# Norms with root and reciprocal per token on partitions, all normalised tiles on VectorE, and the modulation turned in batches

## The chip, the cores and the metric

One core of one Trainium2 chip runs the kernel in one launch. The metric is the device time in microseconds (us); the median of the runs before is 1482.4.

## The reference

Two layers of one trunk work on 256 latent tokens and 256 context tokens of width 1024. Each half of a layer begins with a norm, whose result is modulated; the six modulation vectors of a layer come from two condition vectors (one for latent, one for context tokens):

```python
cond_x = silu(c); cond_c = silu(c_ctx)
for l in range(2):
    mod_x = split(cond_x @ w_mod[l] + b_mod[l], 6)     # 1024 x 6144; mod_c from cond_c alike
    hx = rmsnorm(x, g_norm1[l]) * (1 + mod_x[1]) + mod_x[0]     # hc alike
    px = hx @ w_in[l]       # 3088 columns: mLSTM, differential attention, conv
    x = x + mod_x[2] * (concat(mlstm(px), diff_attention(px), conv(px)) @ w_out[l])
    x = x + mod_x[5] * ffn(rmsnorm(x, g_norm2[l]) * (1 + mod_x[4]) + mod_x[3])
return rmsnorm(x, g_final)
# rmsnorm(x, g) = x * rsqrt(mean(x * x) + 1e-6) * g, the mean over the 1024 features of a token
```

The context stream has the same steps in layer 0 only. ffn is a dense SwiGLU (2816 wide) in layer 0 and a top-2-of-8 router with SwiGLU experts in layer 1.

## The kernel before

Activations are kept with features on partitions: X is 128 x 8 x 512, eight tiles k of 128 features, the first 256 columns the context tokens. Weights come in chunks of 256 columns (1 MB) into a ring of four slots. SyncE issues all loads of the ring in the order of one list (`chunks`), and for chunk n it waits until the last product of chunk n - 4 is through; what stands behind it in the list waits too. Products with the large weights are made from two rounded parts of each operand, three matmuls per product (L523, L818). So a weight chunk must be split before use: ScalarE or VectorE makes the leading part (L1173, L1496), VectorE the remainder (L1497, L1511). There are two buffers for leading parts, so chunk s of the split ones also waits for the products of chunk s - 2.

**A norm** (`norm`, `squared`, `deviation`, `norm_scale`): ScalarE squares each tile (L1058), VectorE sums six of the squares (L1455), TensorE adds them over partitions with two 512-wide matmuls against ones (L567, L569), which puts each token's sum on all 128 partitions. ScalarE takes the root (L1064), VectorE the reciprocal of all 512 columns (L1479). Then VectorE multiplies tiles 0, 2, 4 and 6 (L1469) and GpSimd tiles 1, 3, 5 and 7 (L2097); ScalarE applies gain and shift per half (L1078), VectorE splits the result (L1496, L1497), and TensorE begins the projections (L523) or the router (L880). In layer 1 the second norm covers the 256 latent tokens only.

**The modulation** is 24 chunks per layer. For one chunk TensorE makes 8 matmuls of 256 columns with a 32-column left side in which two columns hold the conditions (L541; 16 records), ScalarE copies the 128 x 256 result to SBUF (L1090), and TensorE turns it into columns with two matmuls against `fold` (L558, the turn; 4 records). VectorE adds the bias (L1438) and makes the gain (L1445). A chunk's turn is issued behind the next chunk's matmuls. Eight chunks come at the start, 16 in layer 0's projections (two behind each of eight weight chunks, `LATE_MOD`), eight in layer 0's attention, four each behind the column sums of the norms (0, 1), (1, 0) and (1, 1), four in layer 1's attention. Attention has 18 steps in layer 0 and 10 in layer 1; `fill` puts modulation into them on TensorE and ScalarE. ScalarE copies the rows of a norm's four chunks before its first tile of that norm.

In the ring's list, a norm's chunks surround the first weight chunk of what follows: two ahead of it, the rest behind it; then "up" (layer 0), or "mq", "cg", "ca" (layer 1). At the start the first weight chunk stands seventh, after six of the eight modulation chunks. `spin` (L530) are matmuls of constants whose result nobody reads; one spin is two records. TensorE runs its instructions in the order written, and so do the others.

After a first norm VectorE splits the tiles, then rounds constants (layer 0 only), clears the scratch, splits "mq" and "cg", waits for ScalarE's gate functions, and does the gate scans (L1533 to L1544) ahead of the remainder of "ca" (`gate_rows`).

## Time and profile before

| | us |
|---|---|
| median of 3 runs | 1482.4 (1482.19 to 1485.1) |
| the profiled execution | 1483.12 |
| its span | 1481.3 |
| TensorE busy | 1401.9 (95%) |
| VectorE busy | 994.1 (67%) |
| ScalarE busy | 642.5 (43%) |
| GpSimd busy | 205.9 (14%) |
| mean granted TensorE clock, of full speed | 0.973 |
| HBM traffic | 266 MB, 180 GB/s over the span |

All times within the kernel are counted from the start of the span. PE is TensorE's matmuls, PEld its weight loads, DVE VectorE, ACT ScalarE, POOL GpSimd, SPq SyncE's queue; L12 is a line of the kernel. A matmul on 32-bit floats appears as two records, one on rounded parts as one. The stages: first modulation and norm to 44, projections of layer 0 to 250, its attention and output to 381, norm to 406, dense stage to 755, layer 1's norm to 773, its projections to 921, attention and output to 995, norm and router to 1027, then eight trips through the experts.

### The profile page before, as it was taken

What the parts mean: (1) busy time and instruction counts of PE and PEld (TensorE: products, weight loads), DVE (VectorE), ACT (ScalarE), POOL (GpSimd) and SP (SyncE); (2) the same over time, 40 slices, a digit from 0 to 9 for tenths busy, and PEclk for the clock granted to TensorE, in tenths of its full rate; (3) what the DMA queues carried; (4) which work ended last, traced back from release to release, by engine and by line L of the source; (5) the groups of instructions that cost most, each with busy time, mean ns of one, the idle gap of its engine ahead of it and who ended that gap; (6) DMA issues with size and microseconds to landing.
All of it is one profiled execution on the core that took longest, in us unless ns stands there. A gap on an engine that the chain in (4) does not pass through costs nothing.

```text
span 1481.3 us, 20769 instructions
## 1 busy us (share of the span) xinstructions
PE 1401.9 (95%) x7796; PEld 1152.9 (78%) x7796; DVE 994.1 (67%) x1456; ACT 642.5 (43%) x1025; POOL 205.9 (14%) x150
## 2 busy tenths in 40 slices
PE   6899999989899999999988999888999999999996
PEld 3778887667688888888868888577888888878885
DVE  3755885565643443444457695755988998998996
ACT  3434334561401100010034444635677677687675
POOL 0129980000100000000011980000000000000000
PEclk9999999889999999999999989998999999999998
DMA  9254442411342322222334122238979778877940
GB/s 398 93 199 171 171 171 86 163 37 61 113 167 85 102 98 86 106 81 104 116 119 158 69 86 90 110 114 339 400 298 367 295 300 339 328 298 312 353 196 28
DMA packets 30882, 267.08 MB, mean 180 GB/s; under 512 B 3424, under 2 KB 3552, under 8 KB 4960
## 3 DMA queue, kind: packets, MB, share of 16 engines
q1 hardware_dynamic: 30816, 266.15, 47.3%
q8 instruction: 47, 0.77, 0.2%
q14 instruction: 19, 0.16, 0.0%
HBM read 265.09 MB, written 1.05 MB: 180 GB/s over the span
## 4 chain that ended last, share of the span: by engine, by line
PE 81%; DVE 9%; ACT 3%; issue 3%; DMA 3%; SPq 0%; DVEq 0%; ACTq 0%
PE ps L523 38%; PE ps L953 17%; PE ps L973 7%; PE ps L818 3%; PE ps L541 3%; PE ps L681 2%; DMA sb_arena<-mod 2%; PE ps L558 1%; PE ps L646 1%; PE ps L530 1%; PE ps L736 1%; PE ps L717 1%; DVE sb_egu_lo L1963 1%; DVE sb_w_lo L1511 1%; DVE sb_ew_lo L1974 1%
## 5 line engine op out<-in xcount | busy, mean ns | idle before, releaser
L523 PE MATMUL ps<-sb_h_hi,sb_w_hi 128*128 128x512 f32 (+1 forms) x640 | 242.4, 379 | 4.9 <-DVE sb_w_lo L1497 3.3
L523 PE MATMUL ps<-sb_h_hi,sb_w_lo 128*128 128x512 f32 (+1 forms) x640 | 240.0, 375 | 0.0
L523 PE MATMUL ps<-sb_h_lo,sb_w_hi 128*128 128x512 f32 (+1 forms) x640 | 240.0, 375 | 0.0
L953 PE MATMUL ps<-sb_egu_lo,sb_h_lo 128*128 128x512 f32 (+1 forms) x384 | 144.6, 377 | 0.0
L523 PEld LDWEIGHTS ps<-sb_h_hi,sb_w_hi 128*128 128x128 f32 x640 | 121.7, 190 | 28.3 <-DVE sb_w_lo L1497 3.9
L1496 DVE CAST sb_w_hi<-sb_arena 128x2048 fp32r<-128x2048 f32 (+1 forms) x38 | 45.5, 1197 | 141.8 <-PE ps L523 113.8
L523 PEld LDWEIGHTS ps<-sb_h_hi,sb_w_lo 128*128 128x128 f32 x640 | 121.5, 190 | 21.7
L523 PEld LDWEIGHTS ps<-sb_h_lo,sb_w_hi 128*128 128x128 f32 x640 | 121.6, 190 | 21.1
L1963 DVE TENSOR_TENSOR sb_egu_lo<-sb_arena,sb_con_r 128x1024 fp32r<-128x1024 f32 x98 | 115.3, 1217 | 15.2 <-ACT sb_con_r L1318 15.1
L1974 DVE TENSOR_TENSOR sb_ew_lo<-sb_arena,sb_ew_hi 128x1024 fp32r<-128x1024 f32 x88 | 107.1, 1217 | 11.5 <-ACT sb_ew_hi L1331 11.5
L2118 POOL TENSOR_SCALAR sb_arena<-sb_arena,sb_small 128x512 f32<-128x512 f32 (+1 forms) x60 | 104.2, 1736 | 5.9
L1331 ACT ACTIVATE sb_ew_hi<-sb_arena 128x1024 fp32r<-128x1024 f32 x88 | 91.7, 1052 | 30.1 <-PE ps L973 30.1
L1291 ACT ACTIVATE sb_arena<-ps 128x512 f32<-128x512 f32 x22 | 13.2, 599 | 202.5 <-PE ps L523 202.4
L1963 DVE TENSOR_TENSOR sb_egu_lo<-sb_arena,sb_x_r 128x1024 fp32r<-128x1024 f32 x82 | 96.5, 1217 | 0.4
L1318 ACT ACTIVATE sb_con_r<-sb_arena 128x1024 fp32r<-128x1024 f32 x96 | 96.0, 1051 | 0.0
L1511 DVE TENSOR_TENSOR sb_w_lo<-sb_arena,sb_w_hi 128x2048 fp32r<-128x2048 f32 x24 | 59.3, 2470 | 50.7 <-ACT sb_w_hi L1173 50.5
L1497 DVE TENSOR_TENSOR sb_w_lo<-sb_arena,sb_w_hi 128x2048 fp32r<-128x2048 f32 (+1 forms) x38 | 85.0, 2236 | 1.3
L953 PE MATMUL ps<-sb_con_r,sb_h_lo 128*128 128x512 f32 (+1 forms) x224 | 82.1, 367 | 3.4 <-DVE sb_egu_lo L1963 3.4
L953 PEld LDWEIGHTS ps<-sb_egu_lo,sb_h_lo 128*128 128x128 f32 x384 | 73.0, 190 | 12.6
L953 PE MATMUL ps<-sb_con_r,sb_hs_lo 128*128 128x512 f32 (+1 forms) x224 | 81.6, 364 | 0.0
L1318 ACT ACTIVATE sb_x_r<-sb_arena 128x1024 fp32r<-128x1024 f32 x80 | 80.1, 1055 | 0.0
L2120 POOL TENSOR_TENSOR sb_arena<-sb_arena 128x512 f32<-128x512 f32 (+1 forms) x60 | 75.8, 1263 | 5.0
(328 smaller groups left out, 3028.0 us busy)
## 6 DMA issues: line engine op xcount, KB each, us to landing
sb_arena<-experts SPq DMA_DIRECT2D x90, 1536.0 KB, 8.5
sb_arena<-mod SPq DMA_DIRECT2D x48, 1024.0 KB, 5.3
sb_arena<-in SPq DMA_DIRECT2D x24, 1024.0 KB, 6.6
sb_arena<-gate SPq DMA_DIRECT2D x11, 1024.0 KB, 4.9
sb_arena<-up SPq DMA_DIRECT2D x11, 1024.0 KB, 4.8
sb_arena<-out SPq DMA_DIRECT2D x8, 1024.0 KB, 5.0
sb_arena<-down SPq DMA_DIRECT2D x8, 1024.0 KB, 4.8
sb_arena<-down SPq DMA_DIRECT2D x4, 768.0 KB, 4.2
```

The source lines that it names most:

```text
L523: ins = pe.matmul(o, left[a], right[b], start=(k == first and n == 0), stop=(k == final and n == len(PRODUCTS) - 1))
L953: ins = pe.matmul(o, x[:, k, :], w[:, span, :], start=(k == 0 and n == 0), stop=(k == KD - 1 and n == 2))
L973: ins = pe.matmul(ps[:, m, :], left[a], right[b][:, m * 512:(m + 1) * 512], start=(f == 0 and n == 0), stop=(f == ET - 1 and n == len(PROD ...
L1318: f(glead[x % 4], experts[:, t, a * HALF:(a + 1) * HALF].rearrange("p (a n) -> p a n", a=4), ACT.Copy)\
L1331: f(ew_hi[:, t % 2, :], experts[:, t, 2 * HALF:], ACT.Copy).then_inc(down_leading, 1)
L1496: settled(v.tensor_copy(hi, x), ("hi", key))
L1497: v.tensor_tensor(lo, x, hi.bitcast(F32), ALU.subtract).then_inc(*dve_done.tick(key))
L1511: v.tensor_tensor(w_lo[:, n % RING], chunk_view(chunk), w_hi[:, c % SPLIT].bitcast(F32), ALU.subtract)\
L1963: v.tensor_tensor(egu_lo[t][:, a * HALF:(a + 1) * HALF].rearrange("p (a n) -> p a n", a=4), experts[:, t, a * HALF:(a + 1) * HALF].rearran ...
L1974: v.tensor_tensor(ew_lo[t][:, :], experts[:, t, 2 * HALF:], ew_hi[:, t % 2, :].bitcast(F32), ALU.subtract).then_inc(down_split, 1)
L2118: g.tensor_scalar(p, u, w[:, j:j + 1], None, ALU.mult).then_inc(*pool_done.tick(("product", l, j)))
L2120: ins = g.tensor_tensor(y, y, p, ALU.add)
```

## The change

The matmuls that sum the squares over partitions become one-column matmuls, which leave the sum of each token on its own partition, one column per block of 128 tokens (two matmuls per block). Root and reciprocal are taken of these four columns (two in the last norm). VectorE multiplies the identity by them, which gives a diagonal per block in `rstd`, and one 512-wide matmul of ones with it (`norm_spread`) puts each token's scale on all partitions, in PSUM. VectorE makes all eight normalised tiles from there, three ahead of its first split and the rest between splits; GpSimd makes none. ScalarE loads its root table right behind the squares.

Modulation chunks go in batches of two to four. The conditions lie in the middle of a wider, otherwise zero field, and each chunk of a batch takes a window of 32 columns of it, so that its two rows fall on rows of their own; the batch adds up in one bank, is copied once and turned once. 48 copies and turns become 20. The batches: four and four at the start, eight of two in layer 0's projections, five of two in layer 0's attention, three chunks in each of the norms (0, 1) and (1, 0), two of two in layer 1's attention, four in the norm (1, 1). In the norms, the spread stands behind the batch's first chunk (and the turn of the batch before, where one is open), and ScalarE copies the rows behind its last tile. In attention one batch stands between the conv's mean and variance as before, the others in steps 2, 6, 10 and 14; the pair ahead of step 0 is gone. The last batch is turned in the router, and VectorE's last modulation stands ahead of its wait for the ranks. At the start the norm's sums stand behind the fourth chunk, its spread behind the fifth, and 18 spins are laid between the chunks where 6 stood (three of them of the norm). The first load of constants takes the identity along.

```diff
-NORM_AFTER = 4
+NORM_AFTER = 3
...
+XN_AHEAD = 3
...
-SPIN = {"first": 3, ("squares", 0, 0): 3, ("squares", 0, 1): 2, ("squares", 1, 0): 2, ("squares", 1, 1): 0,
+SPIN = {("squares", 0, 0): 0, ("squares", 0, 1): 2, ("squares", 1, 0): 2, ("squares", 1, 1): 0,
...
-MOD_ATTENTION = (range(0, 8), range(16, 20))
-MOD_NORM = {(0, 1): range(8, 12), (1, 0): range(12, 16), (1, 1): range(20, MOD_CHUNKS)}
-MOD_ENDS = ((0, FIRST_MOD - 1), (1, FIRST_MOD - 1), (1, 19), (1, MOD_CHUNKS - 1))
-MOD_STAGES = {(0, 2 * FIRST_MOD): "modc_first", (0, 48): "modc", (1, 2 * FIRST_MOD): "modc_first", (1, 40): "modc",
+MOD_BATCHES = ([(0, 0, 4), (0, 4, 4)] + [(0, i, 2) for i in range(8, 24, 2)] + [(1, i, 2) for i in range(0, 10, 2)]
+               + [(1, 10, 3), (1, 13, 3), (1, 16, 2), (1, 18, 2), (1, 20, 4)])
+MOD_SIZE = {(l, i): n for l, i, n in MOD_BATCHES}
+MOD_ATTENTION = ((0, 2, 4, 6, 8), (16, 18))
+MOD_NORM = {(0, 1): 10, (1, 0): 13, (1, 1): 20}
+MOD_ENDS = ((0, 4), (0, 22), (1, 8), (1, 18))
+MOST = max(MOD_SIZE.values())
+SPIN_FIRST = (8, 1, 1, 0, 1, 5, 2, 0)
+MOD_STAGES = {(0, 2 * FIRST_MOD): "modc_first", (0, 48): "modc", (1, 20): "modc_first", (1, 40): "modc",
...
-LATE_MOD = {n: (8 + 2 * j, 9 + 2 * j) for j, n in enumerate(IN_ORDER[2:10])}
+LATE_MOD = {n: 8 + 2 * j for j, n in enumerate(IN_ORDER[2:10])}
+def batch(l, first):
+    return range(first, first + MOD_SIZE[l, first])
...
-NCONST_FIRST = CONST["ident"][0]
+NCONST_FIRST = CONST["mask_f"][0]
...
-        cond = sb("cond", [P, KD, TILE])
+        cond = sb("cond", [P, KD, TILE + 2 * MOST - 2])
...
+        nstat = tiny[:, 184:184 + 2 * NB].rearrange("p (i b) -> p i b", i=2)
...
+            batches = {}
+            def modulation_chunk(l, first, i):
                 w = loaded(("mod", l, i))
-                if i == 0 and l == 0:
+                if (l, i) == (0, 0):
                     pe.wait_ge(*act_done.at("cond"))
-                o = open_bank(("mod", l, i))
+                if i == first:
+                    batches[l, first] = open_bank(("modrow", l, first))
+                o, at = batches[l, first], 2 * (MOST - 1 - (i - first))
                 for q in range(KD // GROUPS):
                     for g in range(GROUPS):
                         k = GROUPS * q + g
-                        ins = pe.matmul(o[g * TILE:(g + 1) * TILE, 0:CHUNK], cond[:, k, :], w[:, k, :],
-                                        start=(q == 0), stop=(q == KD // GROUPS - 1))
+                        ins = pe.matmul(o[g * TILE:(g + 1) * TILE, 0:CHUNK], cond[:, k, at:at + TILE], w[:, k, :],
+                                        start=(i == first and q == 0),
+                                        stop=(i == batch(l, first)[-1] and q == KD // GROUPS - 1))
                 ins.then_inc(*pe_done.tick(("mod", l, i)))
-                if i and (l, i - 1) not in MOD_ENDS:
-                    turn_modulation(l, i - 1)
-                if i == MOD_CHUNKS - 1 or (l, i) in MOD_ENDS:
-                    turn_modulation(l, i)
-            def turn_modulation(l, i):
-                pe.wait_ge(*act_drained.at(("mod", l, i)))
-                if i == 0 and l > 0:
+            def modulation(l, first, between=None):
+                turned = [(x, i) for x, i, _ in MOD_BATCHES if x == l and i < first][-1:]
+                for i in batch(l, first):
+                    modulation_chunk(l, first, i)
+                    if i == first and turned and turned[0] not in MOD_ENDS:
+                        turn_modulation(*turned[0])
+                    if i == first and between:
+                        between()
+                if (l, first) in MOD_ENDS:
+                    turn_modulation(l, first)
+            def turn_modulation(l, first):
+                pe.wait_ge(*act_drained.at(("modrow", l, first)))
+                if first == 0 and l > 0:
                     pe.wait_ge(*dve_done.at(("modc", l - 1)))
-                if i == 0 and l == 0:
-                    pe.wait_ge(sem_con, 16)
+                n = MOD_SIZE[l, first]
+                o = ps[:, 7, 4 * first:4 * (first + n)].rearrange("p (j m s) -> p m j s", m=2, s=2)
+                right = fold[:, 0:2 * n].rearrange("p (j s) -> p j s", s=2)
+                row = modrow[MOD_BATCHES.index((l, first, n)) % 2]
                 for m in range(2):
-                    at = 2 * (2 * i + m)
-                    ins = pe.matmul(ps[:, 7, at:at + 2], modrow[i % 2][:, m * P:(m + 1) * P], fold, start=True, stop=True)
-                ins.then_inc(*pe_done.tick(("modT", l, i)))
+                    ins = pe.matmul(o[:, m], row[:, m * P:(m + 1) * P], right, start=True, stop=True)
+                ins.then_inc(*pe_done.tick(("modT", l, first + n - 1)))
...
-                pe.matmul(o[:, 0:T - lo], ones, squares(l, which)[:, 0, 0:T - lo], start=True, stop=False)
                 pe.wait_ge(*act_done.at(("sq", l, which, KD - 1)))
-                pe.matmul(o[:, 0:T - lo], ones, squares(l, which)[:, KD - 1, 0:T - lo], start=False, stop=True)\
-                  .then_inc(*pe_done.tick(("ssq", l, which)))
-                for i in MOD_NORM.get((l, which), ()):
-                    modulation(1, i)
+                for b in range((T - lo) // P):
+                    for k in (0, KD - 1):
+                        ins = pe.matmul(o[:, b:b + 1], squares(l, which)[:, k, b * P:(b + 1) * P], ones[:, 0:1],
+                                        start=(k == 0), stop=(k > 0))
+                ins.then_inc(*pe_done.tick(("ssq", l, which)))
+                if (l, which) in MOD_NORM:
+                    modulation(1, MOD_NORM[l, which], lambda: norm_spread(l, which))
+            def norm_spread(l, which):
+                lo = low(l) if which else 0
+                pe.wait_ge(*dve_done.at(("ndiag", l, which)))
+                o = open_bank(("nscale", l, which))
+                pe.matmul(o[:, 0:T - lo], ones, rstd[:, 0:T - lo], start=True, stop=True).then_inc(*pe_done.tick(("nscale", l, which)))
...
-                fill(l, 2 - l)
                 scores(1)
                 spin(ps[:, 7, CHUNK:], SPIN["scores", l])
                 for n in range(attention_steps(l)):
                     if 1 < n + 1 < len(units):
                         scores(n + 1)
-                    fill(l, 1 if l else n % 2)
+                    fill(l, int(n % 4 == 2))
...
+                turn_modulation(1, MOD_NORM[1, 1])
...
+                pe.wait_ge(*dve_done.at(("modc_gate", 1)))
...
-                if i == FIRST_MOD - 1:
-                    spin(ps[:, 7, CHUNK:], SPIN["first"])
-                modulation(0, i)
+                modulation_chunk(0, i // 4 * 4, i)
+                if i == 0:
+                    pe.wait_ge(sem_con, 16)
+                if i == 4:
+                    turn_modulation(0, 0)
+                spin(ps[:, 7, CHUNK:], SPIN_FIRST[i])
                 if i == NORM_AFTER:
                     norm(0, 0)
+                if i == NORM_AFTER + 1:
+                    norm_spread(0, 0)
+            turn_modulation(0, 4)
...
+                f(spare, eps, ACT.Sqrt)
             def deviation(l, which):
                 lo = low(l) if which else 0
-                f(spare, eps, ACT.Sqrt)
+                nb = (T - lo) // P
                 o = full(("ssq", l, which))
-                f(rstd[:, 0:T - lo], o[:, 0:T - lo], ACT.Sqrt, scale=1.0 / D, bias=eps)\
+                f(nstat[:, 0, 0:nb], o[:, 0:nb], ACT.Sqrt, scale=1.0 / D, bias=eps)\
                     .then_inc(*act_drained.tick(("ssq", l, which)))
             def norm(l, which):
                 lo = low(l) if which else 0
                 act.wait_ge(*dve_done.at(("modc" if which else "modc_first", l)))
-                for i in MOD_NORM.get((l, which), ()):
-                    modulation_rows(1, i)
                 dst = h2 if lo else hT
                 for k in range(KD):
-                    act.wait_ge(*(pool_done if k % 2 else dve_done).at(("xn", l, which, k)))
+                    act.wait_ge(*(dve_done.at(("xn", l, which, k)) if k < KD - 1 else dve_drained.at(("nscale", l, which))))
                     for s in range(lo // CTX, 2):
                         a = s * SEQ - lo
                         ins = f(dst[:, k, a:a + SEQ], squares(l, which)[:, k, a:a + SEQ], ACT.Identity,
                                 scale=gain[:, l, which, k, s:s + 1], bias=modc[:, l, 24 * which + k, s:s + 1])
                     ins.then_inc(*act_done.tick(("h", l, which, k)))
+                if (l, which) in MOD_NORM:
+                    modulation_rows(1, MOD_NORM[l, which])
             filler = [[(1, i) for i in MOD_ATTENTION[l]] for l in range(DEPTH)]
-            def modulation_rows(l, i):
-                o = full(("mod", l, i))
-                if i >= 2:
-                    act.wait_ge(*pe_done.at(("modT", l, i - 2)))
-                elif l:
-                    act.wait_ge(*pe_done.at(("modT", l - 1, MOD_CHUNKS - 2 + i)))
-                f(modrow[i % 2], o[:, 0:CHUNK], ACT.Copy).then_inc(*act_drained.tick(("mod", l, i)))
+            def modulation_rows(l, first):
+                act.wait_ge(*pe_done.at(("mod", l, batch(l, first)[-1])))
+                o = ps[:, plan.get(("bank", ("modrow", l, first)), 0), :]
+                n = MOD_BATCHES.index((l, first, MOD_SIZE[l, first]))
+                if n >= 2:
+                    x, i, size = MOD_BATCHES[n - 2]
+                    act.wait_ge(*pe_done.at(("modT", x, i + size - 1)))
+                f(modrow[n % 2], o[:, 0:CHUNK], ACT.Copy).then_inc(*act_drained.tick(("modrow", l, first)))
...
-            for i in range(FIRST_MOD):
-                if i == LEAD_FIRST:
-                    lead(("in", 0, IN_ORDER[0]))
-                modulation_rows(0, i)
-                if i == 1:
-                    squared(0, 0)
-                if i == NORM_AFTER - 1:
-                    deviation(0, 0)
+            squared(0, 0)
+            modulation_rows(0, 0)
+            deviation(0, 0)
+            lead(("in", 0, IN_ORDER[0]))
+            modulation_rows(0, 4)
...
-                    .then_inc(*dve_done.tick(("xn", l, which, k)))
+                o = full(("nscale", l, which))
+                ins = v.tensor_tensor(squares(l, which)[:, k, 0:T - lo], X[:, k, lo:T], o[:, 0:T - lo], ALU.mult)
+                if k < KD - 1:
+                    ins.then_inc(*dve_done.tick(("xn", l, which, k)))
+                else:
+                    ins.then_inc(*dve_drained.tick(("nscale", l, which)))
             def split_h(l, which, k):
                 dve.wait_ge(*act_done.at(("h", l, which, k)))
             def norm_scale(l, which):
                 lo = low(l) if which else 0
+                nb = (T - lo) // P
                 dve.wait_ge(*act_drained.at(("ssq", l, which)))
-                settled(v.reciprocal(rstd[:, 0:T - lo], rstd[:, 0:T - lo]), ("rstd", l, which))
-                dve.wait_ge(*pe_done.at(("ssq", l, which)))
-                normalised(l, which, 0)
-                normalised(l, which, 2)
+                settled(v.reciprocal(nstat[:, 1, 0:nb], nstat[:, 0, 0:nb]), ("rstd", l, which))
+                v.tensor_tensor(rstd[:, 0:T - lo].rearrange("p (b q) -> p b q", q=P), ident.unsqueeze(1).to_broadcast([P, nb, P]),
+                                nstat[:, 1, 0:nb].unsqueeze(2).to_broadcast([P, nb, P]), ALU.mult)\
+                    .then_inc(*dve_done.tick(("ndiag", l, which)))
+                for k in range(XN_AHEAD):
+                    normalised(l, which, k)
             def norm(l, which):
-                if (l, which) == (1, 1):
-                    normalised(l, which, 4)
-                    normalised(l, which, 6)
-                    return
                 for k in range(KD):
-                    split_h(l, which, k)
-                    if k in (1, 3):
-                        normalised(l, which, k + 3)
+                    if (l, which) != (1, 1):
+                        split_h(l, which, k)
+                    if k + XN_AHEAD < KD:
+                        normalised(l, which, k + XN_AHEAD)
...
+                modulation(1, 40, 48)
...
-                    modulation(1, 0, 2 * FIRST_MOD)
+                    modulation(1, 0, 20)
                 else:
-                    modulation(1, 2 * FIRST_MOD, 40)
+                    modulation(1, 20, 40)
...
-            def normalised(l, which):
-                lo = low(l) if which else 0
-                pool.wait_ge(*dve_done.at(("rstd", l, which)))
-                pool.wait_ge(*pe_done.at(("ssq", l, which)))
-                for k in range(1, KD, 2):
-                    g.tensor_tensor(squares(l, which)[:, k, 0:T - lo], X[:, k, lo:T], rstd[:, 0:T - lo], ALU.mult)\
-                     .then_inc(*pool_done.tick(("xn", l, which, k)))
...
-                normalised(l, 1)
...
-    put("fold", (i[:, None] % TILE == np.arange(2)[None, :]).astype(np.float32))
+    put("fold", (i[:, None] % TILE == np.arange(2 * MOST)[None, :]).astype(np.float32))
```

## Rows read from the trace of the kernel before

**Rows 1.** The page, part 4: the chain that ended last, by engine.

```profile
PE 81%; DVE 9%; ACT 3%; issue 3%; DMA 3%; SPq 0%; DVEq 0%; ACTq 0%
```

**Rows 2.** Windows: length; busy PE, PEld, DVE, ACT, POOL; clock; DMA share, GB/s.

```profile
85.20:250.00 164.80, 164.70 (x1177) 137.07 (x1178) 114.11 (x171) 60.13 (x105) 111.31 (x61) 1.00 0.44 164
...
250.00:346.00 96.00, 83.47 (x509) 56.79 (x508) 61.46 (x149) 47.19 (x122) 0.00 (x0) 0.88 0.26 93
...
406.20:746.60 340.40, 340.38 (x1502) 281.92 (x1502) 145.75 (x126) 27.44 (x49) 0.00 (x0) 1.00 0.29 104
```

**Rows 3.** The chain, 0 to 50 us: start, length, what.

```profile
31.68 3.37 DVE sb_rstd L1479
...
37.44 3.27 DVE sb_w_lo L1511
...
40.85 1.02 DVE sb_gain L1445
...
44.32 5.72 PE ps L523 x13
```

**Rows 4.** Timeline, 35 to 61 us: PE's last chunk; VectorE's last tile, mq.

```profile
35.45 1.07 PE L541 MATMUL ps<-sb_arena,sb_cond 128*32 128x256 f32 x16
...
52.13 0.69 DVE L1497 TENSOR_TENSOR sb_h_lo<-sb_H,sb_h_hi 128x512 fp32r<-128x512 f32 x1
...
58.33 2.29 DVE L1497 TENSOR_TENSOR sb_w_lo<-sb_arena,sb_w_hi 128x2048 fp32r<-128x2048 f32 x1
```

**Rows 5.** The chain, 85 to 250 us: one turn.

```profile
99.61 0.54 PE ps L558 x4
```

**Rows 6.** Source lines: duration ns min/median/max, first and last start, forms.

```profile
L1469 DVE TENSOR_TENSOR sb_arena<-sb_X,sb_rstd x12: 424/692/1764, 35.1 to 1001.0; 128x512 f32<-128x512 f32 x8, 128x256 f32<-128x256 f32 x4
...
L1847 DVE TENSOR_TENSOR sb_arena<-sb_arena,ps x22: 680/686/689, 414.3 to 635.1; 128x512 f32<-128x512 f32 x22
...
L1273 ACT ACTIVATE sb_tiny<-ps,sb_con x2: 262/262/263, 261.6 to 927.8; 128x4 f32<-128x4 f32 x1, 128x2 f32<-128x2 f32 x1
...
L1090 ACT ACTIVATE sb_tiny<-ps x24: 366/383/402, 8.7 to 1000.0; 128x256 f32<-128x256 f32 x24
```

**Rows 7.** The chain, attention of layer 0: four one-column sums.

```profile
327.75 1.05 PE ps L744 x8
```

**Rows 8.** The chain, second norm of layer 0.

```profile
382.02 0.86 PE ps L569 x2
...
383.94 5.68 DMA sb_arena<-mod
...
391.18 0.98 ACT sb_H L1078 x2
...
394.05 0.35 DVE sb_h_hi L1496
...
394.43 0.69 DVE sb_h_lo L1497
...
395.12 0.60 DVE sb_arena L1469
...
402.62 1.23 DVE sb_w_hi L1496
```

**Rows 9.** The chain, first norm and first projections of layer 1.

```profile
759.10 0.86 PE ps L569 x2
...
773.22 16.46 PE ps L523 x72
...
789.70 4.77 DMA sb_arena<-in
...
803.34 2.30 DVE sb_w_lo L1511
```

**Rows 10.** Windows of L541 in attention: PE and PEld busy, clock, DMA share, GB/s.

```profile
270.00:290.00 20.00, 3.21 (x48) 1.25 (x48) 1.00 0.68 252
...
310.00:330.00 20.00, 0.00 (x0) 0.00 (x0) 0.82 0.00 1
```

30 lines of the change are left out of this document (12 added, 18 removed).

## The prediction

> **What bounds the kernel now.** I read the chain that ended last first. By engine it is TensorE for 81% [rows 1], and the windows by stage show where that is plain work: in the projections of layer 0 and in the dense stage TensorE is busy the whole stretch at the full clock of 2.4 GHz [rows 2], so there only fewer TensorE instructions help. Elsewhere the chain leaves TensorE at four places, which are the four norms. In each the same things follow one another: the sums of squares, a reciprocal over all 512 tokens on all partitions (3.37 us), multiplications by it, ScalarE's gain and shift, the split of each tile into two parts, and the first product. At the start that product comes at 44.32 and runs at half clock (13 records in 5.72 us) [rows 3]; in layer 0's second norm and in layer 1's first, what ends the wait is a modulation chunk from HBM (5.68 us), because ScalarE copies the rows of all four chunks before its first tile [rows 8]. After layer 1's first norm the chain shows one more wait: the weights "cg" are loaded only when the first product is through, at 789.70 [rows 9].
>
> **The norm, as it will run.** From the end of the sums S: root of four columns 0.26 [rows 6], reciprocal of four columns 0.2 (an estimate, from that root), the diagonal 0.69 (priced like any 128x512 product on VectorE [rows 6]), TensorE's spread 0.86 (the same form as today's second wide sum [rows 8]), handing over some 0.1. That is 2.1 instead of 0.7 + 3.37. The column sums are 16 records where four stood; eight take 1.05 [rows 7], so 2.1 against some 2 for the two wide sums: nothing. Then VectorE makes three normalised tiles at 0.60, and alternates: eight splits at 1.06 (0.35 + 0.69 and a wait) and five more tiles at 0.60 [rows 8], 11.5 in all. So the first split is ready at S + 5.0 and the last at S + 15.5. GpSimd's half of the tiles has moved to VectorE; between the splits that is five tiles instead of two, 1.8 more, and it is in these 11.5. What it returns: VectorE's own instructions are no longer stretched while GpSimd runs (the same multiplication takes 0.69 in the median and 1.76 at worst [rows 6], the remainder of the first weights 3.27 where it takes 2.29 later [rows 3, 4]).
>
> The tiles now read the scale from PSUM. I price that at nothing: a product with a PSUM operand takes 0.686, the one from SBUF 0.692 [rows 6]. The Trainium skill, "VectorE: DVE Perf Modes", section on the TRN2 errata, gives VectorE a fixed 120 cycles from PSUM against 58 from SBUF, at 0.96 GHz. By that each 512-wide tile would be 65 ns longer, and an estimate by that page for the 24 wide tiles is 1.6 us less gain, 1455.0 as the time. Its rule speaks against the change; the trace does not bear it out.
>
> **Start.** TensorE's chunk of the last first-stage modulation began at 35.45 [rows 4]; its load or TensorE's order let it start there. Then 1.07 for the chunk, 0.38 for the copy [rows 6], 0.54 for the turn [rows 5], 0.4 for VectorE's two modulation instructions (an estimate: the gain writes 16 columns, and today's 1.02 [rows 3] is mostly GpSimd beside it), a tile on ScalarE 1.0 and its split 1.1 [rows 8]: first product at 39.9. The chunk itself may come sooner: today it stands behind the wide sums, seven turns and the spins, which end just ahead of it; how much sooner its load would let it start no row shows. I take 2.5 sooner, 37.4, an estimate; the row of today is the other end. The norm's branch must be done by then. Even if its root were as late as today (reciprocal at 31.68), tile 3 would be ready at 35.4, the weights' remainder at 37.7, the first product at 40.2. So the gain on the first product is 4.1 to 6.9. The spins end just ahead of it, so TensorE may keep 2.4 GHz: 72 records of 0.229 [rows 9] bring the first products through at 53.9, where today they are through at 63.5 (13 records to 50.0, 59 more at 0.229). But the next weights ("mq") are split by VectorE behind its tiles: today 7.8 after the last tile, at 60.6 [rows 4]; now the last tile's split is at 47.9 and mq ready at 55.7. So **7.8** are gained where mq starts, bounds 4.1 and 9.6.
>
> **Turns.** A turn costs TensorE 0.54 [rows 5]. In layer 0's projections, on a full TensorE, 16 become 8: **4.3**, bounds 2 and 5.
>
> **Attention.** Layer 0 has ten chunks for eight (1.07 each: 3.21 for three [rows 10]) and five turns for eight: 0.5 more. A batch of two stands ahead of ScalarE's table load for the conv's deviation, 1.0 more, of which the removed pair of cold chunks there gives back 0.3: **-1.2**, bounds +2 and -6, for bursts of 2.5 us in one step may delay what waits for that step. Layer 1 keeps four chunks and loses two turns (1.1), pays the same 1.0, waits some 0.2 for its last copy, and two chunks (2.1) move to a step in which TensorE waits for VectorE: **2.0**, bounds 4 and -1.
>
> **Second norm of layer 0.** S is 382.9 [rows 8]; the diagonal is ready inside the first chunk's 1.1, spread from 384.1. Last split 398.6; then VectorE splits the "up" weights (1.23 and 2.29 [rows 8, 4], 3.5) and TensorE goes on at 402.1 where it now does at 406.2 [rows 8, 2]: **4.1**, bounds 3 and 5. The chunk loads (three for four) end before; "up" is freed by the first chunk, some 15 us ahead of its split.
>
> **First norm of layer 1.** S is 760.0 [rows 9]. TensorE has a chunk, a turn, the spread, two chunks and four spins (eight records of 256 columns; 512 take 0.43 [rows 8], so 1.8 in all), and its first product comes at 766.5, not 773.22; 72 records last 16.5: to 782.9 instead of 789.7, 6.7 gained. Then the loads: with three chunks in the gap, the ring slot of "cg" is freed by a modulation chunk and not by the first product. Now: load 4.77, split 3.5, 5.2 of gate work on VectorE, remainder of "ca" 2.30, and "ca" products at 805.7 [rows 9]. New: the last tile's split is at 776.0 (the diagonal's spread waits 0.5 for chunk and turn), mq's at 783.0 (7.8 later as at the start, less the constants rounded only there), cg's at 786.5, gate work 791.7, remainder 794.3. mq and cg (96 records of half the columns) occupy TensorE for 11.0 from 783.0, so it hardly waits. ScalarE's gate instructions, hidden today under load and split, are hidden under the split alone; nothing to 2 us. "ca" now waits for the first product; its load (4.8) and copy end at about 791. **11.3**, bounds 6 and 12.
>
> **Router.** Four turns leave the path (2.2), one turn and a spread of half the width enter it (1.0), all ahead of the eight spins that TensorE runs up to its wait for the choice of experts; the columns' sums cost the same: **0.7**, bounds 0 and 1.4. The eight expert trips are untouched. The waits for the gate's modulation stand on VectorE and TensorE with nothing late behind them.
>
> **Sum.** 7.8 + 4.3 - 1.2 + 4.1 + 11.3 + 2.0 + 0.7 = 29.0. The profiled execution took 1483.12 (span 1481.3), which gives 1454.1; it was 0.7 above the median of the runs shown, 1482.4, so I forecast **1453.4**.
>
> **Rivals.** *The loads don't help* (10%): if cg's split, ScalarE's gate steps or the order of the loads hold "ca" back as now, layer 1's norm gives 6.7 or less and the time is 1458 to 1460. For it: three engines meet there within a microsecond or two. Against: each has its own earlier release.
> *Attention pays* (12%): the bursts cost 1.5 us at each of five steps, 7 to 8 more, 1461. For it: the chain there hops between three engines. Against: the same work is there today, in smaller pieces, and all on the chain.
> *More than forecast* (12%): the attention chunks that stand on the chain vanish behind VectorE, and the start gains its 9.6: 1446.
> *Slower, by the clock* (3%): attention's steps lose their regular filling. Where chunks ran the granted clock was 1.00, where none did 0.82 [rows 10], and over layer 0's attention it is 0.88 with TensorE busy 83.5 us [rows 2]. At 1.2 GHz throughout, those 83.5 would be 83.5 x (0.88/0.5 - 1) = 63 us longer. It decides from 29 us, under half of that; with two thirds of it, and some in layer 1, about 1497. Against: today's late steps have no chunks and kept 0.82. The Trainium skill, "TensorE: Matmul & The Clock Gate", section on HAM oscillation, says that waits for data throttle the array again and what follows starts cold, which is the side of this rival; the first product at half clock agrees.
> *Nothing comes of it* (1%): the norms' chains really wait for something unseen; 1482. The rows leave no room.
> The forecast's own case has 62%, 1449 to 1459.
>
> **Chances and range.** Leaving out the slow case, the empty one and the far tails, the range is 1446 to 1461.5. A measurement of this kernel tells 0.2% (3 us) from nothing. Faster 0.95, same 0.02, slower 0.03.
>
> **What would show it.** Right: four-column reciprocals under 0.2 us; first product near 37.4 and not after 40; TensorE on "up" near S + 19 in layer 0; from S to "ca" 34 us in layer 1 instead of 46; half the turns; nothing on GpSimd in the norms. Wrong: a spread that waits long for the diagonal or behind a chunk not yet loaded; tiles from PSUM well over 0.69; TensorE idle ahead of cg; a mean clock in attention under 0.8.

## The result, and the profile after

The changed kernel takes 1464.65 us in the median of 9 runs (1457.22 to 1471.94); the kernel before took 1482.83 beside it (1476.86 to 1485.18). The ratio is 0.9884, 95% interval 0.9856 to 0.9912. I had forecast 1453.4 and a range of 1446.0 to 1461.5: right in sign, but the gain is some 11 us smaller, and the time lies 3 us above my range. The profiled execution took 1464.65, its span 1462.9. The profile of the changed kernel, part 4, the chain by engine:

```profile
PE 84%; DVE 8%; issue 3%; ACT 3%; DMA 2%; SPq 0%; DVEq 0%; ACTq 0%
```

TensorE's share rose from 81% to 84%; VectorE and DMA have one point less each [rows 1]. Where the gain went stands in this table; each stage runs from the start of its first instruction on TensorE to that of the next stage's, in the two profiled executions (us). The second norm of layer 0 ends where TensorE begins the products of "up", the first norm of layer 1 where it begins those of "ca", and the last stage at the start of TensorE's last instruction.

| stage | before | after | gained | forecast |
|---|---|---|---|---|
| start, to mq's first product | 63.4 | 60.7 | 2.7 | 7.8 |
| to the first conv sum of layer 0 (turns) | 188.7 | 185.7 | 3.0 | 4.3 |
| attention, to the output's first product | 76.7 | 72.4 | 4.3 | -1.2 |
| output | 52.1 | 52.2 | -0.1 | 0 |
| second norm, from the sums to "up" | 25.3 | 22.0 | 3.3 | 4.1 |
| dense stage, from "up" on | 351.8 | 351.8 | 0.0 | 0 |
| layer 1's first norm, from the sums to ca | 47.7 | 39.5 | 8.2 | 11.3 |
| to its conv sum | 116.1 | 114.5 | 1.6 | 0 |
| attention, to the output's first product | 45.5 | 48.4 | -2.9 | 2.0 |
| output | 28.2 | 28.3 | -0.1 | 0 |
| second norm and router, to the first expert product | 31.3 | 28.6 | 2.7 | 0.7 |
| experts and end | 451.4 | 455.6 | -4.2 | 0 |

(63.4 is 50.04, where the 13 records of [rows 3] end, and 59 more at 0.227.) That is 18.5 in the profiles. Five terms missed by 3 us or more: the start, the two attentions in opposite directions, layer 1's norm, and the experts, whose code the change doesn't touch.

The chain of the changed kernel through the start:

```profile
21.49 1.07 PE ps L557 x16
22.56 2.92 PE ps L596 x16
25.48 1.86 PE ps L557 x16
...
29.35 1.71 PE ps L607 x2
...
32.92 2.61 PE ps L542 x10
...
37.59 1.04 PE ps L557 x16
...
39.97 0.18 DVE sb_gain L1484
```

L557 is a chunk, L596 the column sums, L607 the spread, L542 the spins. From the sums to the last but one chunk everything takes up to twice its time (a chunk 1.86 for 1.04, the spread 1.71 for 0.86). The last first-stage chunk starts at 37.59, later than before (35.45 [rows 4]); the gain takes 0.18 instead of 1.02 [rows 3], now with nothing on GpSimd beside it. The windows (busy PE, PEld, DVE, ACT, POOL; clock; DMA) say why:

```profile
24.00:26.00 2.00, 2.00 (x15) 1.76 (x19) 0.18 (x1) 0.26 (x1) 0.00 (x0) 0.50 1.08 442
34.00:36.00 2.00, 2.00 (x20) 1.35 (x22) 1.18 (x1) 0.00 (x0) 0.00 (x0) 1.00 1.01 425
```

TensorE ran at 1.2 GHz (a granted clock of 0.50) from about 23 to 33 us, behind a wait of 2.06 us for the load of chunk 3. The same stands in the chain of layer 1's first norm, behind a wait of 2.4 us for ScalarE's last square:

```profile
744.75 1.92 PE ps L596 x16
746.67 1.74 PE ps L557 x16
...
749.36 1.91 PE ps L607 x2
751.27 3.03 PE ps L557 x32
...
756.22 14.99 PE ps L535 x66
...
781.90 2.30 DVE sb_w_lo L1554
784.25 11.77 PE ps L535 x96
```

The first product comes 11.5 after the sums' start, not the 8.5 of the forecast; the load of cg, which stood on this chain in [rows 9], is gone from it. Layer 0's second norm, in the chain, has no load on it either, and a spread of 1.68:

```profile
371.01 1.93 PE ps L596 x16
...
374.28 1.68 PE ps L607 x2
...
392.99 3.01 PE ps L535 x12
```

The new small instructions, by source line (duration in ns, min/median/max), against [rows 6]:

```profile
L1509 DVE TENSOR_TENSOR sb_H<-sb_X,ps x8: 679/680/687, 751.3 to 760.9; 128x512 f32<-128x512 f32 x8
L1523 DVE RECIPROCAL sb_tiny<-sb_tiny x4: 165/178/178, 25.8 to 976.9; 128x4 f32<-128x4 f32 x3, 128x2 f32<-128x2 f32 x1
```

The reciprocal takes 0.18. A wide tile whose scale is in PSUM takes 0.68, where the one from SBUF took 0.69 [rows 6]: here the trace differs from the rule of the Trainium skill, "VectorE: DVE Perf Modes", section on the TRN2 errata, that I had weighed.

### The profile page after: what moved, and what is told of

Its sections match the earlier page's. It is cut to its first block, busy times and chain, and to the rows that moved or that the text cites. A ratio compares the mean times of both kernels' runs of the same rounds, so it can differ in the third digit from the quotient of the medians.

```text
span 1462.9 us, 20612 instructions
## 1 busy us (share of the span) xinstructions
PE 1395.8 (95%) x7756; PEld 1144.4 (78%) x7756; DVE 982.7 (67%) x1476; ACT 632.6 (43%) x997; POOL 181.1 (12%) x134
## 3 DMA queue, kind: packets, MB, share of 16 engines
q1 hardware_dynamic: 30816, 266.16, 47.7%
## 4 chain that ended last, share of the span: by engine, by line
PE 84%; DVE 8%; issue 3%; ACT 3%; DMA 2%; SPq 0%; DVEq 0%; ACTq 0%
PE ps L535 38%; PE ps L989 17%; PE ps L1009 7%; PE ps L852 3%; PE ps L557 3%; PE ps L716 2%; PE ps L752 1%; PE ps L681 1%; PE ps L771 1%; PE ps L542 1%; DMA sb_arena<-mod 1%; DVE sb_egu_lo L2007 1%; PE ps L584 1%; DVE sb_h_lo L1540 1%; PE ps L762 1%
## 5 line engine op out<-in xcount | busy, mean ns | idle before, releaser
L1539 DVE CAST sb_w_hi<-sb_arena 128x2048 fp32r<-128x2048 f32 (+1 forms) x38 | 45.5, 1197 | 126.0 <-PE ps L535 114.7
L2018 DVE TENSOR_TENSOR sb_ew_lo<-sb_arena,sb_ew_hi 128x1024 fp32r<-128x1024 f32 x88 | 107.1, 1216 | 11.5 <-ACT sb_ew_hi L1373 11.5
```

Of the source, the lines that this page charges most:

```text
L1539: settled(v.tensor_copy(hi, x), ("hi", key))
L2018: v.tensor_tensor(ew_lo[t][:, :], experts[:, t, 2 * HALF:], ew_hi[:, t % 2, :].bitcast(F32), ALU.subtract).then_inc(down_split, 1)
```

## Experiments

Each run is the changed kernel with one edit unless it says otherwise, and each ratio is to the kernel before. The first runs asked whether the three losses are in every execution, and undid or mended one thing each.

**again**: nothing edited.

> The changed kernel once more, nothing edited. Theory A: three things are in every execution of it: TensorE at half clock from about 24 to 33 us of the start, layer 1's attention some 2.9 us longer than before (from the end of its projections to the first product of the output 52.6 against 49.7), and trips of the experts of 54.5 us each instead of 54.1. Theory B: the last two vary from one execution to the next; then the trips may take 54.1 here, or attention 50, and the time is that much less. Ratio to before 0.986 to 0.991.

Measured: 1461.09, ratio 0.986 (0.9839 to 0.9881). The half clock at the start is there again (22 to 32 us). Layer 1's attention took 45.4, as before the change, not 48.4. The trips took 54.5 again. So A holds for the start and the experts, B for the attention. But what this execution saved in its attention it lost just behind it. Windows of layer 1's attention, of its output, and of the norm and router up to the first expert product; first this execution, then the one above:

```profile
897.93:943.36 45.43, 34.56 (x245) 23.55 (x246) 31.72 (x77) 30.02 (x66) 0.00 (x0) 0.96 0.26 94
943.36:973.12 29.76, 27.25 (x200) 26.07 (x201) 16.81 (x36) 7.87 (x14) 0.00 (x0) 0.94 0.31 108
973.12:1003.16 30.04, 25.54 (x196) 20.79 (x197) 12.39 (x55) 11.82 (x25) 0.00 (x0) 0.86 0.79 316
```

```profile
898.78:947.23 48.45, 38.47 (x245) 27.16 (x246) 31.62 (x77) 30.27 (x66) 0.00 (x0) 0.86 0.24 87
947.23:975.48 28.25, 25.75 (x200) 24.57 (x201) 16.80 (x36) 7.87 (x14) 0.00 (x0) 1.00 0.32 115
975.48:1004.08 28.60, 24.03 (x197) 20.38 (x197) 12.38 (x55) 11.74 (x25) 0.00 (x0) 0.92 0.81 327
```

The same code on the same data: the half clock falls into other stages, and the three together take 105.2 and 105.3. In the ten profiles that have layer 1's attention as changed, it took 45.4 (twice), 46.9 to 47.1 (five times) and 48.4 to 48.6 (three times), on average 47.2; the three stages together took 105.2 to 106.9. In the three profiles of the kernel before and its shifted copies the attention took 45.5 to 45.7 and the three stages 105.0 to 105.2.

**warm_start**

```
-SPIN_FIRST = (8, 1, 1, 0, 1, 5, 2, 0)
+SPIN_FIRST = (8, 1, 6, 0, 1, 5, 2, 0)
```

> Five more spins (2.2 us at the full clock) fill TensorE's 2.06 us wait for the load of chunk 3. Theory A (the half clock after that wait is what keeps the start from its forecast): the clock stays full from 18 to 40 us, the column sums take 1.9 instead of 2.99, the spread 0.86 instead of 1.91, first product near 37.7 instead of 42.6, mq's first product near 56 instead of 60.7, and the whole is 4 to 5 us shorter than the changed kernel. Theory B (column sums and the order of the chunks, or the load of the last first-stage chunk, hold it): the first product moves by less than 1.5 and the whole by less than 1.5.

Measured: 1464.38, ratio 0.9881 (0.9859 to 0.9903). The clock was full from 18 to 38 and the first product came at 39.76, where it came at 42.60 and 41.78 in the two executions above, and between 40.2 and 42.6 in all eight profiles with the start as changed; each of the eight has a stretch of half clock there. Its chain:

```profile
22.50 1.88 PE ps L596 x16
...
25.44 9.19 DMA sb_arena<-mod
...
34.68 1.11 PE ps L557 x16
```

A is right about the clock and gave 2 to 3 us of the 5 it asked for: behind the clock stands the load of the last chunk, which is issued when chunk 4 has freed its slot and lands 9.19 later, at 34.6. The first conv sum was 2.0 to 2.9 sooner. In the whole time this is within the spread of the runs.

**load_sooner**: the edit of warm_start, and `NORM_AFTER = 4`.

> The five spins of warm_start, and the norm's sums behind chunk 4, where they stood before the change, and not behind chunk 3. Theory A (the last first-stage chunk is loaded into the slot that chunk 4 frees, so the sums ahead of chunk 4 delayed that load by their 1.9 us): chunk 4 ends near 23.6 instead of 25.4, chunk 7 starts near 32.8 instead of 34.7, first product near 38 instead of 39.8. Theory B (the load is held by the rate of all loads, 15 MB in 38 us, and not by the slot): chunk 7 again at 34.2 to 34.7, first product 39.3 to 39.8. Theory C (chunk 4's own load is late, so that the order changes nothing): chunk 4 starts at 24 or later.

Measured: 1461.76, ratio 0.9866 (0.9837 to 0.9896); first product at 39.98. The chain:

```profile
10.39 14.43 DMA sb_arena<-mod
24.86 1.07 PE ps L557 x16
...
27.01 1.68 PE ps L596 x16
...
34.97 1.04 PE ps L557 x16
```

Not A. C as foreseen: chunk 4 itself isn't loaded before 24.8. So where the sums stand makes no difference here. The trace supports B too. From 8 to 36 us the DMA share is 1.00 to 1.01, at 420 to 422 GB/s, in these profiles and in the kernel before, and the last chunk's load lands at about the same time however early it is issued: issued at 25.4 it lands at 34.6 (warm_start), at 26.8 at 34.4 (again), at 27.4 at 35.1 (the changed kernel). So a first product before some 39 needs fewer or other loads ahead of it, not other instructions (an estimate, from the earliest landing in these profiles, 34.1, and the 5.1 that warm_start takes from the chunk on). The kernel before shows the same load:

```profile
L469 SPq DMA_DIRECT2D sb_arena<-mod x1: 327/327/327, 25.4 to 25.4; - x1
...
DMA to landing us min/median/max: 8.7/8.7/8.7
```

It landed at 34.1, and the chunk ran at 35.45 [rows 4]: with these loads there were 1.3 us to gain on it, not 2.5. This I could have read before I forecast.

**warm_norms**

```
-("squares", 0, 1): 2, ("squares", 1, 0): 2
+("squares", 0, 1): 4, ("squares", 1, 0): 7
```

> The changed kernel with five more spins ahead of the sums of layer 1's first norm, where TensorE waits 2.3 us for ScalarE's last square, and two more ahead of those of layer 0's second norm, where it waits 1.0. Theory A (the clock falls behind that wait, and sums, chunk, turn, spread, chunks and spins at half of it are what I missed in layer 1): full clock from the sums to the first product, first product 8.2 to 8.7 after the sums' start instead of 11.5, ca 37 instead of 39.5; in layer 0 the spread takes 0.86 instead of 1.7, the dense stage 21.2 after the sums instead of 22.0; 2.5 to 3.5 us less in all. Theory B (products of one column each, 16 in a row, let the clock fall by themselves): the clock falls as before, first product 11.2 or more after the sums. Theory C (ScalarE's and VectorE's chain to ca has its own pace): the first product comes sooner, ca does not.

Measured: 1463.12, ratio 0.9858 (0.9828 to 0.9889). The chain of layer 1's norm:

```profile
750.96 1.92 PE ps L596 x16
752.88 1.00 PE ps L557 x16
...
754.42 0.98 PE ps L607 x2
```

The clock stays full there, against B: chunk 1.00 for 1.74, spread 0.98 for 1.91; the remainder of ca is ready 36.2 after the sums' start for 39.4, so not C either. The column sums take 1.92 in both, since in the changed kernel the clock fell only behind them. Of these 3.2 only 1.4 are left at the conv's first sum, as the half clock lasts longer between them (from 851 to 861 us, where the changed kernel has one from 849 to 856). In layer 0 the stage took 22.4 instead of 22.0, and the clock fell all the same: two spins there gave nothing. The whole time shows none of the 2.5 to 3.5 us that A asked for.

**rows_ahead**: in ScalarE's `norm`, `modulation_rows` back ahead of the loop over tiles.

> ScalarE copies the rows of the gap's batch ahead of its normalised tiles again, as before the change (nothing else undone). Theory A (the tiles waited for the last chunk's load and its copy, as the chain of before says): layer 0's second norm waits for the third chunk, from the sums' start to the dense stage 26 to 28 instead of 22.0; layer 1's first norm waits for the third chunk as well, first product 2 to 4 later than 11.5 after the sums; 6 to 9 us longer in all. Theory B (VectorE's chain of splits sets both norms whatever ScalarE waits for): within 1.5 of the changed kernel.

Measured: 1467.54, ratio 0.9915 (0.9894 to 0.9935). Layer 0's norm took 24.05 instead of 22.0, and in layer 1 mq's first product came 29.6 after the sums' start instead of the 27.6 of again. The chain in layer 0:

```profile
374.06 1.96 PE ps L557 x32
...
376.10 0.39 ACT sb_modrow_odd L1134
376.48 0.99 ACT sb_H L1121 x2
```

A in kind, but less: the tiles waited for the chunks and the copy, not for a load, and the whole is 3 to 6 us longer than in the two comparisons of the unedited kernel. The third chunk had landed. That the load itself, which [rows 8] shows in the kernel before, would be on the path again, this run does not show.

**four_chunks**: `MOD_BATCHES` with (1, 10, 2), (1, 12, 4) for (1, 10, 3), (1, 13, 3).

> Two chunks in layer 0's gap and four in layer 1's, as layer 1 had them before; all else as changed. Theory A (the load of cg had waited for the first product because of the fourth chunk): cg is loaded only when the first product is through, ca starts 39.5 us after the first sums ran in layer 1 for the first product at 11.5 to 14, that is some 4 to 6 later than the changed kernel's 39.5, 43.5 to 45.5; the dense stage starts at most 0.5 sooner. Theory B (ScalarE's gate work sets ca anyway, it is on the chain after): ca within 1.5 of the changed kernel's 39.5.

Measured: 1468.55, ratio 0.9924 (0.9899 to 0.995). The chain:

```profile
771.38 4.83 DMA sb_arena<-in
...
787.42 11.77 PE ps L535 x96
```

A: the load of cg is on the chain again, behind the last of 72 products, and ca starts 44.7 after the sums instead of 39.5. So some 5 us of what was gained up to ca are the one chunk fewer in that gap. At the conv's first sum 2.0 of them are left in this profile, which has none of the half clock that the changed kernel has at 849 to 856; by the medians the whole is 4 to 7 us longer.

**fill_back**

```
                 conv_spread(l)
+                fill(l, 1 - l)
                 scores(1)
...
```

(and the same batch in ScalarE's order).

> In layer 0 one batch of two chunks runs behind the conv's spread again, as the pair of cold chunks did before, and the last of the four later batches falls away. Theory A (attention 0 gained 4.3 where I had 1.2 lost, because the pair stood on the chain at half clock with its two turns, 4.2 us, and in the later steps its work lies beside ScalarE's and VectorE's): attention of layer 0, from the first conv sum to the first output product, takes 75.5 to 77 instead of 72.4, and the whole 3 to 4 more. Theory B (the gain is from half the turns and from fewer, larger bursts alone): 73 or less.

Measured: 1466.59, ratio 0.9901 (0.987 to 0.9931); attention of layer 0 74.55. The batch stands on the chain:

```profile
262.37 1.00 PE ps L557 x16
263.37 0.54 PE ps L584 x4
263.90 1.00 PE ps L557 x16
```

That is 2.54, and the attention is 2.2 longer than 72.4. But this execution had one more stretch of half clock in that attention, and two others with the batches unmoved took 74.4 to 74.5 in the same way, so it leans to A and doesn't settle it.

**att1_early**: in layer 1 `fill(l, int(n == 0 if l else n % 4 == 2))`.

> Layer 1's second batch of two modulation chunks runs in attention's step 0, where before the change single chunks ran in steps 0 to 2, and not in step 2. Theory A (layer 1 lost 2.9 because its step 2 lies on the chain while step 0 waits on VectorE and the spins have just kept the clock): attention of layer 1 takes 50 from the end of the projections to the first output product, 2 to 3 us less in all. Theory B (the loss is the clock that falls in the late steps, at 931 and 941, where ScalarE rounds the weights of the output and TensorE waits 2.5): no less, 52 to 55, since the late steps are untouched. Theory C: the loss varies between executions.

Measured: 1464.81, ratio 0.9883 (0.9863 to 0.9903); attention of layer 1 46.2, inside the 45.4 to 48.6 of the unedited ones, which is C. But the output and router behind it took 28.3 and 28.6, the short values of both, and the three stages together 103.1, less than in any of the other ten profiles (105.2 to 106.9). So A may be right by some 2 us; it is one execution, and the whole time doesn't show it.

The next question was the experts. **before_shift** is the kernel before with its memory moved as the change moves it:

```
-("fold", 2), ("ones", P)
+("fold", 2), ("pad", 6), ("ones", P)
...
+        sb("pad", [P, 48])
         modrow_odd = sb("modrow_odd", [P, CHUNK])
```

> The kernel before with nothing but its memory moved as the change moves it: six unused columns after fold in the constants and 48 unused columns behind cond, so that everything behind lies 24 and 216 bytes further on in each partition. Theory A (the changed kernel's expert trips take 54.5 us and not 54.09 because of where its tiles lie): the trips take 54.5 here too, eight of them and the stretches like them give 3 to 4 us more, ratio about 1.002 to 1.003. Theory B (it comes from something else in the changed program, such as the length or order of its instructions): the trips take 54.09.

Measured: 1484.45, ratio 1.0029 (1.0009 to 1.0049), trips of 54.55. A.

**after_aligned** adds `("pad", 10)` ahead of the masks; ones and identity, which lie ahead of it, stay 24 bytes further on.

> The changed kernel with ten unused columns ahead of the masks, so that the masks and what lies behind cond are shifted against before by 64 and 256 bytes, not by 24 and 216. Theory A (where the tiles lie, and that by their distance from a multiple of 64 or 256 bytes): trips of 54.09 again, 3 to 4 us less than the changed kernel. Theory A2 (where they lie, but by something else): another length, or 54.5. Theory B (the instructions): 54.5.

Measured: 1462.76, ratio 0.9878 (0.9851 to 0.9904), trips of 54.12. One trip each, in the windows of the kernel before, the changed kernel, before_shift and after_aligned:

```profile
1136.21:1190.30 54.09, 53.23 (x276) 44.77 (x276) 48.30 (x64) 39.31 (x52) 0.00 (x0) 1.00 0.83 322
```

```profile
1114.19:1168.70 54.51, 53.67 (x275) 44.91 (x276) 48.36 (x64) 39.32 (x52) 0.00 (x0) 1.00 0.83 309
```

```profile
1135.93:1190.48 54.55, 53.70 (x275) 44.91 (x276) 48.39 (x64) 39.32 (x52) 0.00 (x0) 1.00 0.84 320
```

```profile
1115.13:1169.24 54.11, 53.25 (x275) 44.73 (x276) 48.30 (x64) 39.28 (x52) 0.00 (x0) 1.00 0.82 318
```

**shift_32**: `("pad", 8)` behind fold in the kernel before, and nothing else.

> The kernel before with eight unused columns behind fold: all that lies behind is 32 bytes further on. Theory A (a shift that is no multiple of 64 bytes costs the expert trips 0.43 us each, as 24 and 216 bytes did and 64 and 256 did not): trips of 54.5. Theory B (32 bytes are enough of a multiple): 54.09.

Measured: 1485.08, ratio 1.0012 (0.999 to 1.0034), trips of 54.3: between the two. The groups of one trip say which instructions are longer (busy us, mean ns), in the kernel before and in before_shift:

```profile
L953 PE MATMUL ps<-sb_con_r,sb_h_lo 128*128 128x512 f32 x20 | 7.9, 393 | 0.0
```

```profile
L954 PE MATMUL ps<-sb_con_r,sb_h_lo 128*128 128x512 f32 x20 | 8.0, 399 | 0.0
```

In shift_32 the same group is at 393 again, and the one with the parts in x_r, 395 in the kernel before, at 399. Which products are longer depends on the shift; what they have in common isn't found.

**warm_aligned**: warm_start, warm_norms and after_aligned in one.

> The three edits together: five more spins at the wait for chunk 3, more spins ahead of the sums of two norms, and the ten unused columns ahead of the masks. If the three costs found are separate, their gains add: first product near 39.8 and 2 us at the end of the projections, 3 us where ca starts in layer 1, trips of 54.1 instead of 54.5 for another 3.5, together 7 to 9 us less than the changed kernel, 1453 to 1457, ratio to before 0.981 to 0.984. Rival: what the warm stretches give is lost again in the attention stages, whose half-clock stretches differ from one execution to the next; then only the 3.5 of the trips stay, and the ratio is 0.985 to 0.986.

Measured: 1457.84 (1451.93 to 1458.55), ratio 0.9841 (0.9816 to 0.9866). Its trips took 54.1, the experts and all behind layer 1's last sums 481.1 instead of 484.2. I had expected 1453 to 1457, and it lies just above. At the start the clock fell once (27 to 31 us) in spite of the spins, and the first product came at 40.33. In layer 1's norm it stayed full, and TensorE began mq 24.9 after the sums, as in warm_norms, for 27.6. Its median is 7 us under the changed kernel's of the first comparison and 3 under that of again. Its interval still overlaps those of the others: by its stages it is the best version, by the total only probably.

## Why the prediction was off

What the second norm of layer 0 and the first of layer 1 were to give came for the most part, by the mechanisms that I named. What failed is that I priced the path at the full clock that I hoped for, and at the start at a load that I hadn't looked up; that I took layer 1's attention as a gain; and that I put the experts at nothing because their code is the same.

**Start, 7.8 forecast, 2.7 measured.** Two steps failed. "The spins end just ahead of it, so TensorE may keep 2.4 GHz" looked at the first product only; the half clock came 20 us sooner, behind a wait for a load, and stretched chunks, turn, spread and spins. And "I take 2.5 sooner, 37.4" had no row. The trace of the kernel before has the load 1.3 ahead of the chunk, and the best start in any run, warm_start's, has its first product at 39.8. The end that I called the row of today (39.9) was the right one. The first products did run at full clock, as said, and mq came 18.1 behind them (forecast 18.3).

**Turns, 4.3 and 3.0.** Within the bounds 2 to 5.

**Attention of layer 0, -1.2 and +4.3** (72.1 to 72.4 in eight of eleven profiles of the changed kernel and its variants, 74.4 to 74.6 in the other three; 75.2 to 76.7 before). Two terms failed. "0.5 more" charged all the work of the attention to the path, also the chunks that moved to later steps, where it lies beside ScalarE's and VectorE's; and the removed pair was mis-sized. The chain of the kernel before has it with its turns whole, the first chunk and its turn at half clock:

```profile
265.93 1.87 PE ps L541 x16
267.80 0.74 PE ps L558 x4
268.54 1.00 PE ps L541 x16
269.54 0.54 PE ps L558 x4
```

That is 4.15, and the changed kernel's chain has nothing in its place. My sum had the pair at 3.5 (two chunks, two turns and the 0.3 that it "gives back") and charged 2.7 for three chunks more and a turn less in the later steps. With 4.15 and without that charge it comes to +2.1. That the later chunks cost nothing isn't shown by itself, as fill_back only leans that way, and the other 2.2 stay open; the mean clock over this attention is 0.91 after for 0.87 before.

**Second norm of layer 0, 4.1 and 3.3.** From the start of the sums to "up" 22.0 for some 21; the spread at half clock (1.68 for 0.86) is 0.8 of it.

**First norm of layer 1, 11.3 and 8.2.** The mechanism was right: four_chunks puts the load of cg back and takes 5.2. The term that was mis-sized is the first product's "766.5", 8.5 behind the start of the sums: chunk, turn, spread and spins were priced at full clock, ran at half, and it came 11.5 behind. warm_norms, which keeps the clock, has ca's weights ready 3.2 sooner, and with them the 11.3 is there up to ca. The 1.6 that the projections behind ca gave is clock as well: the half clock there lasted 10 us before (869 to 879) and 7 after (849 to 856).

**Attention of layer 1 and router, +2.0 and +0.7, measured -2.9 and +2.7.** Read with the output between them, as the windows of again show that they must be, the three stages took 105.3 for 105.0: 2.7 were forecast and nothing came, and in seven of the ten profiles it was a loss of 0.5 to 1.9 (one of them, rows_ahead, has its edit in this norm too). The step that failed is "two chunks (2.1) move to a step in which TensorE waits for VectorE": with the two turns fewer it was to shorten the attention, and no profile shows it shorter than before by more than 0.1. att1_early, which puts that batch into another step, has the three stages at 103.1, where the forecast comes to 102.3; one execution doesn't show that the step was the cause. The rival of the clock had the right mechanism at a small part of its price: short stretches at half clock, not the whole stage.

In the router my own terms, 2.2 less 1.0, give 1.2 and not the 0.7 that I put down. Of the 2.7, half is turns and chunks; the products and transposes behind them also took less (3.47 and 2.82 for 4.39 and 3.51). That goes with the clock: over the two groups it was 0.65 in the kernel before and 0.82 after. In again, with more half clock in this stage, the router gained 1.3.

**Experts, 0 and -4.2.** "The eight expert trips are untouched" was true of the code only. cond is wider by 192 bytes in each partition and the constants by 24. Over all trips of the two profiles the median is 54.06 before and 54.52 after, and eight times 0.46 are 3.7 of the 4.2. before_shift, which has this shift alone, shows it as the cause.

Together, of the 29.0 forecast the start took away 5.1, attention of layer 1 4.9, the experts 4.2, layer 1's norm 3.1, turns and layer 0's norm 2.1; attention of layer 0 gave back 5.5, the router 2.0 and layer 1's projections 1.6. The errors partly cancelled: without their signs they add up to 28.5, with them to 10.3. That the total came within 11 us is in part luck. Of the signs that I named, the reciprocals, the tiles from PSUM, the turns and the idle GpSimd were as expected. The first product was not: at 42.6 it was beyond the 40 that I had named. "up" began 20.1 behind the sums' end for 19. The 34 us from the sums' end to ca were 37.6 in the changed kernel and 34.3 in warm_norms.

## What to carry to other kernels

Price every TensorE step of a changed order at the clock that the waits ahead of it leave. Where a wait of 2 us for a load or another engine can't be removed, fill it with spins: that turned a 1.91 spread into 0.98. It doesn't always hold (two spins ahead of layer 0's norm gave nothing, and the start of warm_aligned fell again), and part of what it gives can be lost behind it. Before you take a load as sooner, look up when it landed. Read a stage together with those behind it, as the half clock moves between them from one execution to the next. When a change resizes a tile that lies below others, compare the duration of a stage that it doesn't touch, and try a shift by a multiple of 64 bytes. That work on the chain at half clock is worth moving behind another engine's work, even when there is more of it, is what layer 0's attention suggests; it wasn't shown.

## What the runs showed of the hardware

- Moving tiles in SBUF by 24 and 216 bytes made seven of the eight groups of 512-column products in an expert trip 1 to 6 ns longer in the mean, and a trip 54.55 instead of 54.09; by 32 bytes it was 54.3. In these three programs nothing else differs. In the changed kernel 24 and 216 bytes gave 54.5, 64 and 256 bytes 54.12. Why is open.
- A wait of under 1 us can stand ahead of a fall to half clock. Four profiles have a wait of 0.7 to 0.9 us for VectorE's rows of the gates (the wait of L671 in the changed kernel) between 101 and 105 us, behind products without a gap, and the ten others have none. In two of the four (fill_back, with 0.9, and warm_norms, with 0.8) the clock fell some 2 us later; in the other two (att1_early, with 0.9, and load_sooner, with 0.7) and in the ten it stayed at 1.00. From mq to the conv's first sum these two took 189.7 and 189.5, the other two 186.7 and 186.4, and the seven without the wait 185.5 to 185.6. So the fall cost some 3 us. That this wait is its cause is likely, but no run removed it. The windows of fill_back:

```profile
98.00:106.00 8.00, 7.06 (x47) 5.67 (x47) 7.92 (x8) 0.77 (x2) 7.74 (x4) 0.94 0.59 244
106.00:114.00 8.00, 8.00 (x43) 7.26 (x42) 3.28 (x3) 5.60 (x7) 7.64 (x5) 0.63 0.00 0
```

- The spread of a kernel's runs goes with its mean granted clock, which is on record for every run. Of 53 runs of the kernel before, the eight with a clock of 0.967 to 0.970 took 1485.1 to 1490.3, the twelve with 0.977 to 0.981 took 1476.3 to 1479.3; a line through all 53 gives 1.1 us for each 0.001 (correlation -0.92). The changed kernel has 1457.2 at 0.980 and 1471.9 at 0.972. That is why an edit worth 2 or 3 us shows in its stage and not in the total.
- Sixteen records of one-column products take 1.7 to 1.9 us at the full clock (forecast 2.1) and 3.5 at half (the start of warm_norms); the 2.92 in the chain of the changed kernel's start had the fall in its midst.
